# Query and key head norms of a hybrid decoder step, done four heads at a time

## The reference, cut to what matters

```python
p = h @ w_in                      # 2048 -> 6144 columns: q, k, v, B, C, xc
q = rms_norm(q.reshape(b, t, 8, 2, 64), g_q)
k = rms_norm(k.reshape(b, t, 8, 2, 64), g_k)
# rms_norm: x * rsqrt(mean(x * x) + 1e-6) * g, mean over the 64 values of a half
o = attention(q, k, v)            # two softmaxes per head and their difference
x = x + concat(rms_norm(o) * 0.8, B * conv3(C * xc)) @ w_out
x = x + experts(rms_norm(x))      # 32 experts, top group, top 2 in it, SwiGLU
```

## Time and profile before

| | |
|---|---|
| median of three runs | 1435.9 us |
| lowest, highest | 1434.64, 1437.3 us |
| the profiled execution's own time | 1436.35 us |
| its span, first to last instruction | 1434.4 us |
| TensorE busy | 1242.1 us, 87% of the span |
| VectorE busy | 433.2 us, 30% |
| ScalarE busy | 217.4 us, 15% |
| moved from and to HBM | 496.42 and 6.59 MB, 351 GB/s over the span |

### The profile page before, as it was taken

How to read it: one execution, slowest core, us unless ns; L and a number is a source line. 1 busy time by engine, 2 the same in 40 slices (tenths; PEclk the granted TensorE clock), 3 DMA queues, 4 the chain that set the end, 5 groups by cost and what they waited for, 6 DMA issues and landing times.

```text
span 1434.4 us, 21171 instructions
## 1 busy us (share of the span) xinstructions
PE 1242.1 (87%) x8998; PEld 675.9 (47%) x8998; DVE 433.2 (30%) x863; ACT 217.4 (15%) x462; POOL 45.4 (3%) x33
## 2 busy tenths in 40 slices
PE   9999999999999998997877778796787787777887
PEld 8888888888788862331222232132232122213223
DVE  4322127674211143322311321231222231132142
ACT  3111232322000043110101111011011010101101
POOL 0000003140000001000000000000000000000000
PEclk9999999999999999998989998899999898999899
DMA  9975443669399359999999999999999999999997
GB/s 342 348 227 183 140 133 121 206 206 340 88 349 413 121 182 427 417 425 435 427 433 432 430 433 431 431 431 431 431 432 432 430 432 432 432 432 430 433 426 317
DMA packets 101202, 503.63 MB, mean 351 GB/s; under 512 B 9294, under 2 KB 79638, under 8 KB 86182
## 3 DMA queue, kind: packets, MB, share of 16 engines
q1 hardware_dynamic: 89346, 494.86, 85.0%
q10 hardware_dynamic: 11812, 8.14, 1.8%
HBM read 496.42 MB, written 6.59 MB: 351 GB/s over the span
## 4 chain that ended last, share of the span: by engine, by line
PE 53%; DMA 44%; DVE 2%; ACT 1%; issue 0%; DVEq 0%; ACTq 0%; SPq 0%
PE bank L735 31%; DMA ring<-in_w_gate 16%; DMA ring<-in_w_up 15%; DMA ring<-in_w_down 12%; PE bank L1023 9%; PE bank L1058 3%; PE bank L958 2%; PE bank L1076 1%; DVE xa L1913 1%; PE bank L1073 1%; DMA xa<-in_x_prompt 1%; PE bank L746 0%; PE bank L826 0%; PE bank L776 0%; PE bank L1084 0%
## 5 line engine op out<-in xcount | busy, mean ns | idle before, releaser
L1023 PE MATMUL bank<-ring,bc 128*32 128x512 f32 x2040 | 272.4, 669 | 113.7 <-DMA ring<-in_w_gate 61.9
L735 PE MATMUL bank<-bc,ring 128*128 128x264 f32 x1536 | 350.8, 387 | 1.3 <-ACT cat L1261 1.3
L735 PEld LDWEIGHTS bank<-bc,ring 128*128 128x128 f32 x1536 | 288.2, 190 | 51.5 <-issue 2.3
L1023 PEld LDWEIGHTS bank<-ring,bc 128*32 128x32 f32 x2040 | 63.7, 118 | 288.2 <-issue 146.5
L1913 DVE TENSOR_TENSOR xa<-xa,bank 128x512 f32<-128x512 f32 x128 | 79.3, 682 | 153.0 <-PE bank L1076 146.6
L735 PE MATMUL bank<-cat,ring 128*128 128x264 f32 x512 | 114.9, 387 | 0.0
L735 PEld LDWEIGHTS bank<-cat,ring 128*128 128x128 f32 x512 | 97.0, 190 | 17.7 <-issue 1.3
L1927 DVE COPY bc<-bank 128x512 f32<-128x512 f32 x32 | 22.1, 691 | 234.6 <-PE bank L1023 234.6
L1058 PE MATMUL bank<-ring,cat 128*32 128x512 f32 x480 | 67.2, 684 | 22.4 <-DMA ring<-in_w_down 22.4
L958 PE MATMUL bank<-cat,bc 128*32 128x512 f32 x512 | 61.3, 597 | 13.5 <-DVE xa L1913 13.5
L1487 ACT ACTIVATE bc<-bank 128x512 f32<-128x512 f32 x32 | 19.1, 597 | 289.6 <-PE bank L1023 289.6
(11 more groups left out here) (300 smaller groups left out, 1023.5 us busy)
## 6 DMA issues: line engine op xcount, KB each, us to landing
ring<-in_w_gate SPq DMA_DIRECT2D x27, 4096.0 KB, 31.8
ring<-in_w_up SPq DMA_DIRECT2D x27, 4096.0 KB, 31.6
ring<-in_w_down SPq DMA_DIRECT2D x26, 4096.0 KB, 32.7
ring<-in_w_in SPq DMA_DIRECT2D x23, 2048.0 KB, 15.3
ring<-in_w_up SPq DMA_DIRECT2D x10, 2048.0 KB, 12.9
ring<-in_w_gate SPq DMA_DIRECT2D x9, 2048.0 KB, 15.4
ring<-in_w_down SPq DMA_DIRECT2D x9, 2048.0 KB, 16.1
ring<-in_w_out SPq DMA_DIRECT2D x8, 2048.0 KB, 16.5
```

Of the source, the lines that this page charges most:

```text
L735: m = pe.matmul(bank[n % 3][:, 0:T], w[:, k, (i % TPU) * P:(i % TPU + 1) * P], src[:, k, :], start=n_k == 0, stop=n_k == KT - 1)
L1023: m = pe.matmul(bank[b][c * C:(c + 1) * C, :], xeT[j % 2][:, k, :], wx, start=i == 0 and x < 4, stop=i == 1 and x >= 4, skip_group_check=True)
```

## The change

The norm is done for four heads at a time (`NORM = 4`), and the rows follow four tiles later.

- VectorE copies each q and k tile raw out of PSUM into `qkT` (`copy_raw`), which frees the bank; ScalarE squares from `qkT` into one of four buffers.
- After tiles n = 4, 8, 12 and 16 TensorE sums the squares of the four heads before (`half_sums(g)`): four products with 32 columns of `blk` (16 of each half), one in each column group, all in bank 3. Head x of the four then has its two sums on partitions 32x to 32x + 31.
- One root and one reciprocal, in place, serve the four heads.
- After tiles n = 5, 9, 13 and 17 TensorE spreads the factors (`widen(g)`): four products of 32 rows by 128 columns with a 0/1 matrix `wide`, one in each row group, into banks 5, 6, 7 and 3. `wide` is built once by VectorE at n = 1.
- VectorE multiplies the four heads with gain and factor, in place in `qkT`, reading the factors from PSUM.
- `rows` and `rows_outgoing` run at n = 6 to 29 and no more at n = 2 to 25, in the order of `ROW_TILES`: q heads, k heads 0 to 3, v heads at the same n as before, and k heads 4 to 7 last, at n = 26 to 29. The product of the sample queries and new keys (`self_scores`) goes from n = 17 to n = 19 on VectorE.

```diff
+NORM = 4
+ROWS0 = NORM + 2
+ROW_TILES = [*range(H + NORM), *range(2 * H, 3 * H), *range(H + NORM, 2 * H)]
+WIDE_BANKS = (5, 6, 7, 3)
...
-            def half_sums(t):
-
-                pe.wait_ge(squared, t + 1)
-                if t == 0:
+            def half_sums(g):
+
+                pe.wait_ge(squared, NORM * g + NORM)
+                if g == 0:
                     pe.wait_ge(consts2_in, 16)
-                if t >= 1:
-                    pe.wait_ge(rooted, t)
-                pe.matmul(bank[3][:, 0:T], const("blk"), sq[t % 2], start=True, stop=True).then_inc(summed, 1)
+                    pe.wait_ge(raw_copied, 2)
+                else:
+                    pe.wait_ge(qk_ready, NORM * g)
+                for x in range(NORM):
+                    m = pe.matmul(bank[3][C * x:C * x + C, 0:T], const("blk")[:, HALF - 16:HALF + 16], sq[x],
+                                  start=True, stop=True, skip_group_check=True)
+                m.then_inc(summed, 1)
+
+            def widen(g):
+
+                pe.wait_ge(inverted, g + 1)
+                for x in range(NORM):
+                    rows_ = slice(C * x, C * x + C)
+                    m = pe.matmul(bank[WIDE_BANKS[x]][:, 0:T], wide[rows_, :],
+                                  rstd[rows_, :], start=True, stop=True)
+                m.then_inc(widened, 1)
...
-                if 1 <= n <= 2 * H:
-                    half_sums(n - 1)
-                if 2 <= n < 3 * H + 2:
-                    rows(n - 2)
+                if n % NORM == 0 and NORM <= n <= 2 * H:
+                    half_sums(n // NORM - 1)
+                if n % NORM == 1 and NORM < n <= 2 * H + 1:
+                    widen(n // NORM - 1)
+                if ROWS0 <= n < ROWS0 + 3 * H:
+                    rows(n - ROWS0)
...
             def square(t):
-                act.wait_ge(tile_done, t + 1)
-                if t >= 2:
-                    act.wait_ge(summed, t - 1)
-                A(sq[t % 2], bank[t % 3][:, 0:T], ACT.Square).then_inc(squared, 1)
-
-            def root(t):
-                act.wait_ge(summed, t + 1)
-                if t >= 2:
-                    act.wait_ge(qk_ready, t - 1)
-                A(rstd[t % 2], bank[3][:, 0:T], ACT.Sqrt, bias=const("eps")).then_inc(rooted, 1)
+                act.wait_ge(qk_raw, t + 1)
+                A(sq[t % NORM], qkT[:, t, :], ACT.Square).then_inc(squared, 1)
+
+            def root(g):
+                act.wait_ge(summed, g + 1)
+                if g >= 1:
+                    act.wait_ge(widened, g)
+                A(rstd, bank[3][:, 0:T], ACT.Sqrt, bias=const("eps")).then_inc(rooted, 1)
...
+            def copy_raw(t):
+
+                dve.wait_ge(tile_done, t + 1)
+                V.tensor_copy(qkT[:, t, :], bank[t % 3][:, 0:T]).then_inc(qk_raw, 1)
+
+            def invert(g):
+
+                dve.wait_ge(rooted, g + 1)
+                V.reciprocal(rstd, rstd).then_inc(inverted, 1)
+
+            def normalise(g):
+
+                dve.wait_ge(widened, g + 1)
+                for x in range(NORM):
+                    t = NORM * g + x
...
+                    V.scalar_tensor_tensor(qkT[:, t, :], qkT[:, t, :], gqk[:, t // H:t // H + 1], bank[WIDE_BANKS[x]][:, 0:T],
+                                           ALU.mult, ALU.mult).then_inc(qk_ready, 1)
```

More of the change, by code:

```diff
@@ L217, in build @@
         ord_ = tmp[:, 1560:1816]
-        sq = [tmp[:, 1296 + T * i:1296 + T * i + T] for i in range(2)]
+        sq = [tmp[:, T * i:T * i + T] for i in range(NORM)]
         diff = tmp[:, 1824:2208]
         diffT = tmp[:, 2208:2592]
-        rstd = [tmp[:, 1824 + T * i:1824 + T * i + T] for i in range(2)]
+        rstd = tmp[:, 1824:1824 + T]
+        wide = tmp[:, NORM * T:NORM * T + P]
         ctmp = tmp[:, 2592:2592 + T]
@@ L370, in build @@
         squared = sem("squared")
+        qk_raw = sem("qk_raw")
+        inverted = sem("inverted")
+        widened = sem("widened")
         summed = sem("summed")
@@ L737, in tile, with rows @@
                 m.then_inc(tile_done, 1)
-            def half_sums(t):
-                pe.wait_ge(squared, t + 1)
-                if t == 0:
+            def half_sums(g):
+                pe.wait_ge(squared, NORM * g + NORM)
+                if g == 0:
                     pe.wait_ge(consts2_in, 16)
-                if t >= 1:
-                    pe.wait_ge(rooted, t)
-                pe.matmul(bank[3][:, 0:T], const("blk"), sq[t % 2], start=True, stop=True).then_inc(summed, 1)
-            def rows(t):
+                    pe.wait_ge(raw_copied, 2)
[12 more added lines that the diff above has]
+                m.then_inc(widened, 1)
+            def rows(r):
+                t = ROW_TILES[r]
                 src = qkT[:, t, :] if t < 2 * H else vT[t % 2]
@@ L754, in rows @@
                     pe.wait_ge(v_copied, t - 2 * H + 1)
-                if t >= 1:
-                    pe.wait_ge(rows_out, t)
+                if r >= 1:
+                    pe.wait_ge(rows_out, r)
                 if t >= H:
@@ L768, in head_scores @@
             def head_scores(h):
-                pe.wait_ge(qk_ready, H + h + 1)
+                if h == 0:
+                    pe.wait_ge(qk_ready, 2 * H)
                 if h >= 1:
@@ L1316, in copy_v, with rows_outgoing @@
                 if h >= 2:
-                    act.wait_ge(rows_T, t - 1)
+                    act.wait_ge(rows_T, V_ROW0 + h - 1)
                 A(vT[t % 2], bank[t % 3][:, 0:T], ACT.Copy)
                 A(vTs[:, h * NB:(h + 1) * NB], bank[t % 3][:, SEQ:T], ACT.Copy).then_inc(v_copied, 1)
-            def rows_outgoing(t):
-                stage, s = kvstage[t % 2], stored[t % 2]
+            def rows_outgoing(r):
+                t = ROW_TILES[r]
+                stage, s = kvstage[r % 2], stored[r % 2]
                 cols = slice((t % H) * HD, (t % H + 1) * HD)
-                act.wait_ge(rows_T, t + 1)
+                act.wait_ge(rows_T, r + 1)
                 if t < H:
@@ L1361, in _ @@
             for n in range(NIN):
+                if n % NORM == 0 and NORM <= n <= 2 * H:
+                    root(n // NORM - 1)
                 if n < 2 * H:
@@ L1371, in _ @@
                     A(ctmp, bank[n % 3][:, 0:T], ACT.Copy).then_inc(c_copied, 1)
[L1372 to L1375, removed]
+                if ROWS0 <= n < ROWS0 + 3 * H:
+                    rows_outgoing(n - ROWS0)
                 h, stage = divmod(n - HEAD0, 3)
@@ L1580, in _ @@
             st.do(V.tensor_tensor(lamv[:, 0:1], lamv[:, 0:1], const("c0"), ALU.add))
[L1582 to L1588, removed]
+            def copy_raw(t):
[8 more added lines that the diff above has]
+                    t = NORM * g + x
+                    if x == 0:
+                        dve.wait_ge(squared, NORM * g + NORM)
+                        dve.wait_ge(qk_raw, NORM * g + NORM)
+                    V.scalar_tensor_tensor(qkT[:, t, :], qkT[:, t, :], gqk[:, t // H:t // H + 1], bank[WIDE_BANKS[x]][:, 0:T],
+                                           ALU.mult, ALU.mult).then_inc(qk_ready, 1)
             prev = prevT.rearrange("p (b j i) -> p b j i", b=NB, j=2)
@@ L1707, in _ @@
             for n in range(NIN):
-                if 1 <= n <= 2 * H:
-                    normalise(n - 1)
+                if n == 1:
+                    dve.wait_ge(consts2_in, 16)
+                    st.do(V.tensor_copy(wide.rearrange("p (c d) -> p c d", c=2),
+                                        const("fold")[:, 0:C:16].unsqueeze(2).to_broadcast([P, 2, HALF])))
+                g, stage = divmod(n - NORM, NORM)
+                if stage == 1 and 0 <= g < 2 * H // NORM:
+                    invert(g)
+                if n < 2 * H:
+                    copy_raw(n)
+                if stage == 1 and 0 <= g < 2 * H // NORM:
+                    normalise(g)
                 if n == 2 * H + 1:
@@ L1712, in _ @@
                     dve.wait_ge(raw_copied, 2)
+                if n == 2 * H + 3:
                     dve.wait_ge(qk_ready, 2 * H)
```

11 lines of the change are left out of this document (6 added, 5 removed).

## The result

The changed kernel took **1445.76 us** (median of five runs, 1444.93 to 1446.19) against 1436.57 us of the kernel before (five runs beside it, 1434.64 to 1439.42): a ratio of 1.0061, 95% interval 1.005 to 1.0072. It is 9.2 us slower. The forecast was 1434.8, with 1437.2 as the upper end of its range: it is wrong by far more than the runs scatter.

What follows compares the result with a forecast made beforehand. TensorE's own work was taken to bound the front stage, saturated transfers the expert stage. Removing 7.1 us and adding 6.0 saves 1.1, with waits and moves at 0: from the 1435.9 median, 1434.8 us, range 1432.3 to 1437.2.

Steps and rivals of the forecast that it cites:

- the sum for TensorE: Front stage: 7.1 us of norm products removed, 6.0 us of column and row groups added, so 1.1 us less.
- column group: Front stage, `half_sums`: four products running at once, 0.65 us per group, 0.10 more where a 128-column load follows.
- row group: Front stage, `widen`: four products in row groups, 0.75 us per group, with 0.10 or 0.01 behind it.
- waits costed at 0: Front stage: TensorE's waits for squares, root, reciprocal, factors and normed rows were taken as covered by slack, 0 us.
- The end of the root's chain at n = 27: Front stage: without rows in front, the difference ends 7.42 us after the scores instead of 8.15.
- 0.44 of slack: At n = 27 the turn's weights load 0.44 us behind the difference's end; about 0.04 would remain, wait at most 0.4.
- 0.09 on either side: Array-shape changes on TensorE: the trace was said to show 0.09 us at both entry and exit of a group.
- moving the front stage forward moves the stream with it, one to one: Front stage to expert-weight stream: time saved reaches the end, since the sync queue waited 80.7 us for TensorE's tiles.
- the one on the other side: Rival, front stage: groups overlap only in pairs, 2.5 us slower, 1438.4 us; chance 0.06.
- nothing arrives: Rival: a wait at n = 28 and the entry to the expert stage take the saving back, 1435.9 us; chance 0.12.

Runs made afterwards that it cites:

- e2: Changed kernel with three wide warm-up products instead of thirteen, 40 instructions fewer: 1435.92 us against 1437.6 of the kernel before (0.9989).
- e12: Same kernel as e2, measured again in five rounds: 1436.72 us against 1437.16 of the kernel before (0.9994).
- e3: Changed kernel with 128 TensorE instructions more ahead of the loop (three wide, 42 tiny warm-up products): 1437.43 us against 1437.6 of the kernel before (1.0001).
- e8: Changed kernel with 20 instructions fewer (three wide, five tiny warm-up products): 1444.72 us, a single execution.
- e1: Kernel before with twelve tiny products behind the warm-up, 48 instructions more, nothing of the change: 1447.42 us against 1437.6 (1.0069).
- e11: Changed kernel with 256 instructions more (three wide, 74 tiny warm-up products): 1449.28 us, a single execution.
- e5: Kernel before with seven wide products ahead of each expert-loop pass and three wide warm-up products for thirteen: 1435.95 us against 1436.41 (0.9995).
- e6: Kernel before with nine loads of a single 15,360-byte row into one partition per pass of the sync queue's loop: 1478.12 us against 1436.41 (1.0285).
- e7: Kernel before with the added products of e5 and the single-row loads of e6 together: 1477.47 us (1.029).
- e13: Kernel before with nine loads per pass of the sync queue's loop, each sixteen rows of 960 bytes: 1446.51 us against 1437.45 (1.0061).
- e4: Kernel before with nine DRAM-to-DRAM copies of 16,384 bytes per pass of the sync queue's loop, 54 in all: 1439.09 us against 1437.6 (1.0013).
- e9: Kernel before with one load of nine 15,360-byte rows per pass of the sync queue's loop: 1452.05 us against 1437.16 (1.0096).

## Why the prediction was wrong

**Right: the sum for TensorE.** The steps of 0.90 and 0.97 us less the normal 0.22 make 0.68 for a column group and 0.75 for a row group (0.65 and 0.75 forecast). The lead at 495 us is 0.90 of the 1.1 forecast; the very first tile, ahead of any norm, starts 0.18 us later in the changed kernel's trace (14.03 for 13.85), so from there TensorE gains 1.08. The rows give 0.09 us at the entry to a group and 0.10 for the unhidden load behind it; the "0.09 on either side" of the prediction is a loose reading of them, without effect on the sum. None of the waits costed at 0 came. The end of the root's chain at n = 27 fell as worked out. The turn L809 loads its weights 0.06 us behind the difference's end (240.80 + 0.34), so the 0.44 of slack was used up and not exceeded:

```profile
240.80 0.34 DVE L1673 SCALAR_TENSOR_TENSOR xa<-xa,small 128x128 f32<-128x128 f32 x1
241.20 0.14 PEld L809 LDWEIGHTS bank<-consts,xa 128*128 128x128 f32 x1
```

**Right as far as it went: "moving the front stage forward moves the stream with it, one to one".** The lead was 0.91 us at 708 us, and where the code stays in place (e2, e12) the end is earlier by 1.7 and 0.4 us.

**Wrong: the step that took everything outside the front stage as untouched.** The sum counted the products that the change adds, by their time only, 1.1 us less of it, and held the expert stage fixed because no line of it changes. The products are also code. Here 45 more instructions stand ahead of a loop whose last block had room for at least 5 and fewer than 25 more. The fetches that follow load the DMA engines unevenly and so delay the last share of the last load: a term of +9.6 us beside the -1.1 of the sum. None of my rivals had it: the one on the other side priced overlap in pairs, 2.5 us, and "nothing arrives" looked for waits. The range of 1432.3 to 1437.2 was as wide as the doubts inside the front stage and had nothing for one outside it. What could have been read from the trace of before: in the page's part 3 a row for the fetching of code, 33 packets, and their end at 726 us while the loop went on, hence a loop that just stays in TensorE's instruction memory. The size of its body against whole blocks was in the compiled program.

## What to carry to other kernels

When a change adds or removes instructions ahead of a loop, count them on that engine and ask which blocks the loop's code then spans; the packets of the instruction queue in the profile tell at once whether it is fetched in every pass. A loop that nearly fills an engine's instruction memory can be put right by moving it either way, with a few warm-up products fewer (e2) or with padding (e3), so test a small change to such a kernel in two positions before judging it. And in a stage where the weights' stream is saturated, price an extra transfer by what it does to the stream's packets and to the most burdened DMA engine, not by its bytes: 0.83 to 0.9 MB cost 1.9, 9.1, 9.6, 14.9 or 41.7 us here.

## What the runs showed of the hardware

- **TensorE's code.** A loop of 1664 instructions (6.5 blocks of 256) is kept where it spans seven blocks and fetched anew in each pass where it spans eight, nine packets of 1.08 us each (1.14 in e8), with a stop at its head of 5.6 us (33.3 us in six, the changed kernel) to 6.3 us (37.8 in six, e8).
- **The fetches load about half of the DMA engines.** With them eight of sixteen work at the stream for 11.7 to 12.6 us after the others are through (changed, e1, e8, e11), without them for 1.7 (before).
- **Some 6 us of extra work of TensorE in each pass are free** in a stage where it already waits up to 7.8 us for the stream (e5; with the rows of e6 as well in e7).
- **Small loads into partitions of SBUF disturb the stream** more than copies from DRAM to DRAM: 0.83 MB in rows of 960 bytes cost 9.1 us (e13), 0.88 MB of copies in packets of 1,024 bytes 1.9 (e4). What it is in the loads that does this stays open.
- **The clock at the first tiles.** In the profiled executions of e1, e2, e9 and e13 TensorE was granted 0.57 to 0.58 of its clock (near the lower of its two levels, 1.2 for 2.4 GHz) from 14 to 18 us; in the other eleven, those of the kernel before and of the changed one among them, 1.00. It is not the kernel: e12 is the same as e2, and e9 and e13 have the warm-up of before. Nor does the work just ahead differ: from 12 to 14 us TensorE was busy 0.68 to 0.82 us in these four and 0.69 in the kernel before. Four microseconds at 0.57 are 1.7 us of work less, and the first 100 MB of the stream were through that much later: at 460.4 to 460.7 us in e1, e9 and e13 for 458.8 before, and at 459.3 in e2 for 457.6 in e12. Stretch 14 to 18 us of e1, columns as in rows 2:

```profile
14.00:18.00 4.00, 3.86 (x10) 3.11 (x11) 4.00 (x11) 0.28 (x2) 0.00 (x0) 0.57 1.09 345
```

  The runs of one kernel scatter by somewhat more (1434.8 to 1440.1 in 25 runs of the one before). Whether this is the cause of that scatter was not tried.
